# The adaLN modulation products of a two-layer hybrid block: full array against four column quarters

## The reference

```python
c_s = jax.nn.silu(c)
cc_s = jax.nn.silu(c_ctx)
for layer in range(DEPTH):
    mod = (c_s @ ada_w[layer] + ada_b[layer])[:, None, :]
    sh1, sc1, g1, sh2, sc2, g2 = jnp.split(mod, N_MOD, axis=-1)
    modc = cc_s @ ada_w[layer] + ada_b[layer]
    hl = rmsnorm(x, norm_mix_w[layer]) * (1.0 + sc1) + sh1
    hc = rmsnorm(xc, norm_mix_w[layer]) * (1.0 + scc1) + shc1
    ...
```

## Time and profile before

| | us |
|---|---|
| median of 3 runs | 4340.61 |
| lowest, highest | 4338.54, 4340.88 |
| the profiled execution | 4338.09 |
| its span | 4336.4 |

### The profile page before, as it was taken

One profiled execution on the slowest core, in us unless ns is written; L12 is line 12 of the kernel. 1 busy time (PEld: TensorE's weight loads), 2 busy tenths in 40 slices (PEclk: granted clock), 3 DMA queues, 4 the chain that ended last, 5 costly groups with the idle time before them and its releaser, 6 DMA issues. The chain is left out here.

```text
span 4336.4 us, 58553 instructions
## 1 busy us (share of the span) xinstructions
PE 3656.8 (84%) x20572; PEld 2969.4 (68%) x20572; DVE 1614.9 (37%) x2708; ACT 1087.8 (25%) x1931; POOL 726.3 (17%) x850
## 2 busy tenths in 40 slices
PE   4999447787787999999997997546796779999998
PEld 1887331666675788888885886432685657888886
DVE  1311766265333322222224211765363333222224
ACT  2210441154122211211213111530361222211122
POOL 0010656232300000000000111756222100000000
PEclk9999558888879999999998998558898799999999
DMA  5121767422610111111111222765406211111111
GB/s 178 61 83 62 251 220 259 115 63 63 178 44 20 34 39 39 39 39 39 34 39 41 85 83 87 241 221 173 121 21 176 84 33 44 48 48 48 48 48 59
DMA packets 247136, 390.83 MB, mean 90 GB/s; under 512 B 106483, under 2 KB 146931, under 8 KB 244086
## 3 DMA queue, kind: packets, MB, share of 16 engines
q1 hardware_dynamic: 233974, 344.74, 25.5%
q0 software_dynamic: 13056, 44.74, 2.8%
HBM read 282.88 MB, written 106.51 MB: 90 GB/s over the span
## 5 line engine op out<-in xcount | busy, mean ns | idle before, releaser
L392 PE MATMUL ffn_bank<-ffn_h_hi,ffn_w_hi 128*128 128x512 f32 (+1 forms) x1760 | 651.5, 370 | 53.5 <-DVE ffn_h_lo L246 53.5
L395 PE MATMUL ffn_bank<-ffn_h_lo,ffn_w_hi 128*128 128x512 f32 (+1 forms) x1760 | 650.6, 370 | 0.0
L396 PE MATMUL ffn_bank<-ffn_h_hi,ffn_w_lo 128*128 128x512 f32 (+1 forms) x1760 | 649.9, 369 | 0.0
L392 PEld LDWEIGHTS ffn_bank<-ffn_h_hi,ffn_w_hi 128*128 128x128 f32 x1760 | 334.0, 190 | 111.8 <-issue 40.3
L341 PE MATMUL prj_acc<-prj_w_hi,prj_h_hi 128*128 128x472 f32 x960 | 364.1, 379 | 44.0 <-DVE prj_h_lo L246 44.0
L396 PEld LDWEIGHTS ffn_bank<-ffn_h_hi,ffn_w_lo 128*128 128x128 f32 x1760 | 333.7, 190 | 55.9
L395 PEld LDWEIGHTS ffn_bank<-ffn_h_lo,ffn_w_hi 128*128 128x128 f32 x1760 | 334.1, 190 | 55.2
L341 PE MATMUL prj_acc<-prj_w_hi,prj_h_lo 128*128 128x472 f32 x960 | 364.8, 380 | 0.0
L353 POOL DMA_DIRECT2D proj<-prj_out x120 | 65.3, 544 | 1783.7 <-ACT prj_out L299 1508.8
L341 PE MATMUL prj_acc<-prj_w_lo,prj_h_hi 128*128 128x472 f32 x960 | 362.1, 377 | 0.0
L386 DVE TENSOR_TENSOR ffn_w_lo<-ffn_raw,ffn_w_hi 128x1024 fp32r<-128x1024 f32 x132 | 161.8, 1226 | 518.4 <-ACT ffn_w_hi L382 513.2
(11 more groups left out here) (309 smaller groups left out, 6182.3 us busy)
## 6 DMA issues: line engine op xcount, KB each, us to landing
ffn_raw<-w_ffn SPq DMA_DIRECT2D x132, 512.0 KB, 3.5
slv_m_w<-ada_w SPq DMA_DIRECT2D x20, 2048.0 KB, 8.0
pack<-pre_pk SPq DMA_DIRECT2D x20, 1536.0 KB, 5.3
proj<-prj_out POOLq DMA_DIRECT2D x120, 236.0 KB, 2.3
prj_raw<-w_in SPq DMA_DIRECT2D x96, 236.0 KB, 4.5
pre_pr<-proj SPq DMA_DIRECT2D x20, 768.0 KB, 4.4
scn_fd<-feat SPq DMA_DIRECT2D x40, 384.0 KB, 3.8
feat<-pre_ft SPq DMA_DIRECT2D x20, 512.0 KB, 2.7
```

The lines of the kernel that those rows point to most:

```text
L392: mm = pe.matmul(out, w_hi, b_hi, start=first, stop=False)
L395: pe.matmul(out, w_hi, b_lo, start=False, stop=False)
L396: return pe.matmul(out, w_lo, b_hi, start=False, stop=last)
```

## The change

The eight products of a turn's half are dealt to four column quarters of the array, two to each: `k` = 2 x quarter + step. A quarter writes its two rows at partitions 32 x quarter of `acc[u]`, so the bank holds four partial sums of two rows each. ACT copies all 128 partitions into `rows`, which has now 128 partitions. The banks are set to zero once, on DVE, ahead of everything (`clear`), and PE waits for that (`cleared`). The transposes become products: stationary a [128, 128] block of `rows`, moving a [128, 2] matrix `pick` with ones at partitions 32 x quarter + v, which adds the four partial sums and turns the rows into columns at once. POOL makes `pick` from the identity with four small operations at the start of its part of the modulation (`gpsimd`), and PE waits for them (`picked`). In `solve`, `clear` comes ahead of DVE's substitution.

```diff
-    rows = st.sb("m_rows", [2, TURNS * DM])
+    rows = st.sb("m_rows", [P, TURNS * DM])
+    pick = st.sb("m_pick", [P, 2])
-    acc = [st.ps(f"m_acc{u}", [2, 512]) for u in range(2)]
+    acc = [st.ps(f"m_acc{u}", [P, 512]) for u in range(2)]
+    cleared, picked = st.sem("m_cleared"), st.sem("m_picked")
+    QUARTERS = 4
+
+    def clear(eng):
+        for u in range(2):
+            eng.memset(acc[u][:], 0.0).then_inc(cleared, 1)
...
     def tensor(pe):
         pe.wait_ge(silu_done, 1)
+        pe.wait_ge(cleared, 2)
...
-                for k in range(KC):
-                    mm = pe.matmul(acc[u][:], c_s[:, k, :], w[u][:, k, :], start=(k == 0), stop=(k == KC - 1))
+                for step in range(KC // QUARTERS):
+                    for quarter in range(QUARTERS):
+                        k = quarter * (KC // QUARTERS) + step
+                        mm = pe.matmul(acc[u][32 * quarter:32 * quarter + 2, :], c_s[:, k, :], w[u][:, k, :],
+                                       start=(step == 0), stop=(step == KC // QUARTERS - 1), tile_position=(0, 32 * quarter))
                 mm.then_inc(acc_done[u], 1)
         for u in range(2):
             pe.wait_ge(row_done[u], TURNS)
+        pe.wait_ge(picked, QUARTERS)
         for m in range(NM):
-            mm = pe.transpose(cols[:, 2 * m:2 * m + 2], rows[:, m * P:(m + 1) * P], ident[0:2, 0:2])
+            mm = pe.matmul(cols[:, 2 * m:2 * m + 2], rows[:, m * P:(m + 1) * P], pick[:], start=True, stop=True)
         mm.then_inc(turned, 1)
 
     def gpsimd(pool):
+        pool.tensor_copy(pick[:], ident[:, 0:2]).then_inc(picked, 1)
+        for quarter in range(1, QUARTERS):
+            pool.wait_ge(picked, quarter)
+            pool.tensor_tensor(pick[:], pick[:], ident[:, 32 * quarter:32 * quarter + 2], ALU.add).then_inc(picked, 1)
         pool.wait_ge(small_in, 16 + 32 * len(parts))
         pool.wait_ge(cols_out, 1)
...
@@ solve @@
             @block.vector
             def _(dve):
+                clear(dve)
                 substitute(dve, 0)
```

More of the change, by code:

```diff
@@ L101, in modulation @@
     with Stage(nc, "ada") as st:
-        sync, scalar, tensor, gpsimd = modulating(nc, st, parts, cs, ada_w, ada_b, norms, ident, mods)
+        sync, scalar, tensor, gpsimd, clear = modulating(nc, st, parts, cs, ada_w, ada_b, norms, ident, mods)
         with nc.Block() as block:
+            block.vector(clear)
             block.sync(sync)
@@ L181, in gpsimd @@
         pool.wait_ge(scale_done, len(parts))
-    return sync, scalar, tensor, gpsimd
+    return sync, scalar, tensor, gpsimd, clear
 def normed(nc, st, x, scale, mod, shift0, lo, hi_t, lo_t, ones, eps, bufs=None, ms=None):
@@ L1005, in solve @@
         half = 2 * TILES
-        sync, scalar, tensor, gpsimd = beside(st)
+        sync, scalar, tensor, gpsimd, clear = beside(st)
         with nc.Block() as block:
```

## The result

| | kernel before | kernel after |
|---|---|---|
| median of 16 runs each | 4338.59 us | 4349.02 us |
| lowest, highest | 4331.90, 4344.61 | 4340.88, 4353.48 |
| the profiled execution, its span | 4338.09, 4336.4 | 4342.56, 4340.9 |

The ratio of after to before is 1.0023, with a 95% interval of 1.0016 to 1.0031: 10.4 us slower by the medians. The forecast had been 8.9.

The account below looks back on a forecast made before the run. Time is a sum of barrier-closed stages: PE and its loads bound M, the modulation S0, the stores S1. M -4.5, S0 -2.2 and S1 +15.6 give +8.9 us on the 4340.61 median: 4349.5 us, range 4336 to 4353.

Parts of the forecast that it names:

- M: Modulation ahead of layer 0: weight products end at 52.6 instead of 63.06, column products take 7.0 us; -4.5 us.
- The overlap of quarters: Weight products: four quarters run side by side, 4 records in sequence per load instead of 16; 3.6 us at half level.
- Rivals 3 and 4: Weight products: quarters overlap only by twos (+10.9 us, chance 0.08), or not at all (+39 us, chance 0.03).
- S0: Solve of layer 0: POOL with its stores ends it instead of the weights, then `pick` and column products; -2.2 us.
- the loads would be hidden: Solve of layer 0: the last load is through at about 725, before POOL's substitution ends at 727.53.
- S1: Solve of layer 1: `pick` and 32 column products, hidden before, now follow the last store; +15.6 us.
- The price and clock of the column products: Turning of the rows: two records a product, 0.2145 us each at half level; 7.0, 20.7 and 13.9 us.
- Rival 1: Column products in the three stages raise the clock; -3.1 us in all, 4337.5 us, chance 0.15.
- PE will not have such a stretch again; I take half level: Weight products: PE lacks 5.6 us of unbroken work, so the clock stays at half, 3.6 us a load.
- The range: Whole kernel: 4336 to 4353 us; M's clock and the 14 us of stores leave 3 us either way.

Follow-up runs that it names:

- e3: Kernel after with the two loops of the weight products exchanged, quarter by quarter; M 38.6, S0 118.4, S1 111.1 us.
- e6: Kernel before with its transposes made as ordinary fp32 products; M 46.3, S0 135.1, S1 95.9 us.
- e9: Kernel after with PE repeating weight products while it waits for `pick`, 17 in S0, 44 in S1; M 36.4, S0 114.5, S1 109.3 us.
- e1: Kernel after with `pick` formed ahead of POOL's substitution in `solve`; 4319.31 us against 4342.06 for the kernel before, ratio 0.9946.
- e7: e1 with each half's column products made right behind its weight products, loop written out; 4301.97 us against 4342.06 for the kernel before, ratio 0.9911.

## Why the prediction was right

The time came out at 4349.0 for a forecast of 4349.5, and 10.4 us slower by the medians for a forecast of 8.9. That the two times meet within 0.5 us is in part luck: the forecast was added to a median of 3 runs, 4340.61, which lay 2.0 above the later median of 16, and the change itself came out 1.5 larger by the medians. The stages are the better test: +7.8 measured for +8.9. Step by step:

- **M, -4.5 forecast, -4.0 measured.** The last weight product was to end at 52.6 and ended at 53.4: the terms of the chain held (3.6 us a load at half level, the waits for landings), but the third load was 0.2 late and the fourth landed at 49.76, 5.9 behind the third and not 5.3. The column products took 6.96 for 7.0.
- **The overlap of quarters**, taken as 4x from halves and quadrants: 3.59 to 3.62 us a load. Right, and e3 bears out the reason given for it, that the order of issue doesn't tie the tiles to each other. Rivals 3 and 4 are out.
- **S0, -2.2 forecast, -3.0 measured.** `pick` forms right behind the stores, PE starts 1.16 us after it, the 96 records take 20.6 for 20.7. Of the 0.8 us, 0.5 lie in POOL's time up to the stores' landing (95.85 us into the stage for 96.35). That the loads would be hidden held by little: their end, forecast 79.9 us into the stage and 2.5 ahead of POOL's substitution, came at 81.9 and 0.2 ahead.
- **S1, +15.6 forecast, +14.75 measured**: 1.15 to PE, 13.79 for 13.9, 0.4 for ACT and POOL as forecast. The rest, some 0.6, is again POOL's earlier arrival (95.66 us into the stage, 96.26 before).
- **The price and clock of the column products**, 216 ns a record at half level from L948 (the sum itself uses 214.5, with no row of its own): measured 213, and e6 and e9 show that they don't hold even a full level. The prediction's own evidence was thinner than it says: the level had fallen by 767, but the 3.09 us of transposes ran at full, have 0.95 up to 766.9, and PE had been idle since 765.66. The fall under unbroken work is shown by e6 and e9 only. Rival 1 rested on their being ordinary products and not transposes; the runs speak against it three times.
- **"PE will not have such a stretch again; I take half level"** for the weight products was half wrong. In S0 the level changed back and forth, the mean over the loads was 0.66:

```profile
652.00:718.00 66.00, 35.65 (x180) 4.37 (x184) 63.49 (x50) 6.57 (x11) 62.06 (x51) 0.66 0.97 345
```

Single loads took 1.90 to 3.59 us. It cost the forecast nothing, since the loads were hidden in S0 and S1, and in M three of four ran at half level. In other executions of M it did matter: in e1's the weights ended 2.3 us earlier in the stage and the column products were 2.0 us shorter. So M's agreement to 0.5 us is partly luck too.

- **The range** of 3 us either way for M's clock and the stores covered what the kernel after showed; M alone differed by 4.3 us in e1's execution. That the sum lay on the 0.2% bound was said; the measured interval, 1.0016 to 1.0031, lies across it too.

## What to carry to other kernels

An operand that another engine prepares belongs ahead of everything in that engine's queue, not at the start of the function that happens to deal with it: four operations of 0.2 us behind a wait for stores made a hidden step cost 15 us, and moving them up gave back 28 in the two solves. Before speeding up an engine, ask which stage is bound by it at all, and what serial step follows it there; here column tiles cut a load's products to a quarter of their time, and the kernel was 10 us slower for it; it was 23 us faster than before once `pick` came first (e1), and 40 once the step behind the products was also spread into the gaps that they had opened (e7). A short moving operand makes an fp32 product a pair of weight loads: 0.22 us of a full stationary tile at full clock, 0.43 at half, against 0.06 to 0.11 for a transpose.

## What the runs showed of the hardware that was not expected

- Four column quarters with two stationary columns each run fully side by side in fp32, in both orders of the products tried (after, e3): 3.6 us for 16 records of 512 columns at half level, and 1.9 at full (after, e7).
- PE can fall to half level without idling: in e9 some 4.5 us (S0) and 5 us (S1) into the column products, which followed the repeated products without a gap, and in e6 1.9 us into them, behind a gap of 0.86 us.
- Shorter weight products left PE idle for longer between the loads, and it came to the next step at half level (quarters: busy 13.9 of 21.4 us) and not at full (halves: busy 18.0 of 23.3). That step took 3.3 us more. This is one execution of each, and with quarters as well part of it ran at full level in e1 and e9.
- The profile's clock column reads 1.00 from the start of the execution until the first fall that it has on record, here at 44.4, also where the records go at half-level pace (16 of them in 3.56 us). Early in a trace the records' own length is the safer sign.
